# Seven-product fours in the down layers of an fp32 transformer kernel, and fours and turned chunks later in the gate/up loop

## The reference, cut to what matters

```python
def swiglu(x, w_gate, w_up, w_down):
    return (jax.nn.silu(x @ w_gate) * (x @ w_up)) @ w_down

x = x + 0.5 * swiglu(rmsnorm(x, g1), ffn1_w_gate, ffn1_w_up, ffn1_w_down)   # 2048 -> 5632 -> 2048
x = x + hybrid_mixer(rmsnorm(x, g2), ...)
x = x + 0.5 * swiglu(rmsnorm(x, g3), ffn2_w_gate, ffn2_w_up, ffn2_w_down)
return rmsnorm(x, g4)
```

## Time and profile before

| | |
|---|---|
| median of 3 runs | 2597.78 us (2594.83 to 2601.99) |
| the profiled execution's own time | 2595.44 us |
| its span | 2593.6 us |
| TensorE (PE) busy | 2576.0 us, 99% |
| VectorE (DVE) busy | 1765.2 us, 68% |
| ScalarE (ACT) busy | 1258.1 us, 49% |
| granted TensorE clock | 1.00 |
| moved by DMA | 561.53 MB, mean 217 GB/s |

### The profile page before, as it was taken

One profiled execution on the slowest core, in us unless ns is written; L12 is line 12 of the kernel. 1 busy time (PEld: TensorE's weight loads), 2 busy tenths in 40 slices (PEclk: granted clock), 3 DMA queues, 4 the chain that ended last, 5 costly groups with the idle time before them and its releaser, 6 DMA issues.

```text
span 2593.6 us, 32729 instructions
## 1 busy us (share of the span) xinstructions
PE 2576.0 (99%) x11549; PEld 2128.6 (82%) x11549; DVE 1765.2 (68%) x2077; ACT 1258.1 (49%) x1464; POOL 203.1 (8%) x345
## 2 busy tenths in 40 slices
PE   9999999999999999999999999999999999999998
PEld 8888888888788888888888888888888787888887
DVE  7766665887888865556655665555678888885554
ACT  5544554554555544444444644444454545454333
POOL 0122110000000000001100420000100000000000
PEclk9999999999999999999999999999999999999999
DMA  7788785667676776668876677665766667677654
GB/s 218 251 262 231 213 246 181 195 218 222 210 229 218 221 225 210 209 209 263 240 215 191 190 232 216 207 209 192 228 215 216 210 225 215 222 221 240 194 192 158
DMA packets 280067, 561.53 MB, mean 217 GB/s; under 512 B 22826, under 2 KB 25784, under 8 KB 279720
## 3 DMA queue, kind: packets, MB, share of 16 engines
q1 hardware_dynamic: 257120, 489.61, 60.7%
q0 software_dynamic: 22208, 70.19, 9.0%
q10 hardware_dynamic: 648, 0.52, 0.1%
HBM read 526.02 MB, written 34.22 MB: 216 GB/s over the span
## 4 chain that ended last, share of the span: by engine, by line
PE 50%; issue 42%; DMA 4%; POOL 2%; DVE 1%; ACT 0%; SPq 0%; DVEq 0%; ACTq 0%; POOLq 0%
PE acc L661 44%; DMA turn_dram<-h_turned 2%; POOL h_back L574 1%; PE acc L780 1%; PE acc L773 1%; PE acc L776 1%; PE s_ps L880 1%; DMA turn_dram<-turned_s 1%; PE o_ps L904 1%; POOL back_s L574 1%; DMA h_back<-turn_dram 0%; PE tr L796 0%; DVE wlo L1672 0%; DMA raw<-in_ffn_w_gate 0%; DMA qk<-turn_dram 0%
## 5 line engine op out<-in xcount | busy, mean ns | idle before, releaser
L1672 DVE TENSOR_TENSOR wlo<-raw,whi 128x1024 fp32r<-128x1024 f32 (+1 forms) x929 | 1098.4, 1198 | 643.0 <-ACT whi L1197 634.3
L1197 ACT ACTIVATE whi<-raw 128x1024 fp32r<-128x1024 f32 (+1 forms) x929 | 950.8, 1036 | 928.3 <-PE acc L661 659.4
L661 PE MATMUL acc<-whi,act_hi 128*128 128x512 f32 (+1 forms) x1280 | 348.5, 393 | 0.1
L661 PE MATMUL acc<-whi,act_lo 128*128 128x512 f32 (+1 forms) x1280 | 341.2, 388 | 0.0
L661 PE MATMUL acc<-wlo,act_hi 128*128 128x512 f32 (+1 forms) x1280 | 340.9, 388 | 0.0
L773 PE MATMUL acc<-whi,act_hi 128*128 128x512 f32 x1040 | 288.3, 390 | 1.6 <-ACT whi L1197 1.6
L780 PE MATMUL acc<-wlo,act_hi 128*128 128x512 f32 x1040 | 289.1, 390 | 0.7 <-DVE wlo L1672 0.2
L776 PE MATMUL acc<-whi,act_lo 128*128 128x512 f32 x1040 | 287.7, 389 | 0.0
L661 PEld LDWEIGHTS acc<-whi,act_lo 128*128 128x128 f32 x1280 | 239.2, 188 | 50.4 <-DVEq L1801 0.4
L661 PEld LDWEIGHTS acc<-wlo,act_hi 128*128 128x128 f32 x1280 | 239.3, 188 | 49.8
L661 PEld LDWEIGHTS acc<-whi,act_hi 128*128 128x128 f32 x1280 | 234.7, 188 | 44.8 <-issue 0.3
(11 more groups left out here) (335 smaller groups left out, 2324.5 us busy)
## 6 DMA issues: line engine op xcount, KB each, us to landing
raw<-in_w_in SPq DMA_DIRECT2D x280, 512.0 KB, 4.5
raw<-in_ffn_w_gate SPq DMA_DIRECT2D x176, 512.0 KB, 4.6
raw<-in_ffn_w_up SPq DMA_DIRECT2D x176, 512.0 KB, 4.3
raw<-in_ffn_w_down SPq DMA_DIRECT2D x176, 512.0 KB, 4.7
raw<-in_w_out SPq DMA_DIRECT2D x64, 512.0 KB, 4.6
turn_dram<-h_turned POOLq DMA_DIRECT2D x25, 512.0 KB, 2.9
h_back<-turn_dram POOLq DMA_DIRECT2D x100, 128.0 KB, 4.9
raw<-in_w_sg_out SPq DMA_DIRECT2D x24, 512.0 KB, 3.7
```

Source lines behind the costliest of these rows:

```text
L661: return nc.tensor.matmul(pair[:, half, 0:width], left[:, j * TILES + t, half * P:(half + 1) * P], right[:, (first_group + j) % RING, t, 0 ...
L1197: nc.scalar.activation(whi[:, slot, tiles, 0:width], source[:, tiles, 0:width], ACT.Copy).then_inc(hi_ready, 1)
L1672: nc.vector.tensor_tensor(wlo[:, slot, tiles, 0:width], split_source(m)[:, tiles, 0:width], whi[:, slot, tiles, 0:width].bitcast(F32), ALU ...
```

## The change

1. `CHUNK_ORDER`: five left, four 0, one left, one right, four 1, five right (again 20 groups). `turned_hi` and `turned_lo` of the loop move from j == 5 to j == 16 (`TURNED_AT`).
2. The down layer's four units become two pairs, (0, 1) and (2, 3), of 56 groups in `DOWN_ORDER`. k-pairs 0 to 5 of both are fours, with one left and one right group between two fours; k-pairs 6 to 21 are plain. In all, 32 plain groups and 6 fours a pair.
3. The down layer's combined activations are made in the first pair: on VectorE `combine` at j = 0, 2, 4 (two fours each) and their low part (`combined_lo`) at j = 1, 3, 5, the rounding on ScalarE (`round_four`) at j = 1, 3, 5. The last hidden chunk is split at j == 8 in place of 5.
4. At the last four of a pair `fours_out` runs, and the new `fours_added` adds its two results to `xres`; `residual_out` follows after the left part and after the right part.
5. In the first layer the exchanged chunks of x are split at j = 4 and 47 of the second pair and at j == 1 of the mixer's first unit, before TensorE's own transposes there (j == 3), and GpSimd's two loads for the layer norm (`ln_g`, `ln_b`) wait until the third of them is split. In the second layer the first three units' statistics are gathered at the group after the left part of the last pair.
6. Bookkeeping (`KINDS`, `kind_of`, `LOADS_BEFORE`) is rewritten for the two orders.

```diff
-CHUNK_ORDER = ([("left", k) for k in range(2, 6)] + four(0) + [("left", 6), ("left", 7)] + four(1)
-               + [("right", k) for k in range(2, G_D)])
+CHUNK_ORDER = ([("left", k) for k in range(2, 7)] + four(0) + [("left", 7), ("right", 2)] + four(1)
+               + [("right", k) for k in range(3, G_D)])
+TURNED_AT = len(CHUNK_ORDER) - 4
+DOWN_PAIRS = KF // TILES
+DOWN_FOURS = 6
+DOWN_ORDER = ([("left", k) for k in range(6, 12)] + [("right", k) for k in range(6, 12)] + four(0))
+for _k in range(1, DOWN_FOURS):
+    DOWN_ORDER += [("left", 11 + _k), ("right", 11 + _k)] + four(_k)
+DOWN_ORDER += [("left", k) for k in range(17, DOWN_PAIRS)] + [("right", k) for k in range(17, DOWN_PAIRS)]
...
 # GpSimd
             pool.dma_start(mfix[:], mix_fixed).then_inc(mfix_in, 16)
+            pool.wait_ge(chunk_split, 4 + 3 + 4 + 4 + FF_CHUNKS + 3)
             pool.dma_start(ln_g, sg_ln_g_2[:, :].partition_broadcast(P)).then_inc(ln_in, 16)
...
 # TensorE, ffn
-                for c in range(CHUNKS):
-                    for j in groups(KF // TILES, h_hi, h_lo, ends_by_half=4 if not first_one and c == CHUNKS - 1 else 0):
...
+                for c in (0, 2):
+                    for j in paired(DOWN_ORDER, h_hi, h_lo, down_hi, down_lo,
+                                    ends_by_half=4 if not first_one and c else 0):
+                        if c == 0 and j == 3:
+                            h_turns()
+                        if c == 0 and j == 11:
+                            pe.wait_ge(four_ready, (1 if first_one else 2 + DOWN_FOURS // 2) + DOWN_FOURS // 2)
+                        if c == 0 and j == LAST_CHUNK - 1:
                             chunk_is_split()
+                if first_one:
+                    exchanged(2)
...
             for j in groups(G_D, act_hi, act_lo):
                 if j == 3:
+                    exchanged()
+                    chunk_is_split()
                     transpose_chunk(xres, 3 * W)
...
 # ScalarE
+            def round_four(dest, source):
+                rounded[0] += 1
+                act.wait_ge(four_summed, rounded[0])
+                nc.scalar.activation(dest, source, ACT.Copy).then_inc(four_rounded, 1)
...
+                for c in (0, 2):
+                    for j in paired(DOWN_ORDER):
+                        if c == 0 and j in (1, 3, 5):
+                            if j == 1:
+                                act.wait_ge(group_used, DOWN_AT[0 if first_one else 1])
+                            round_four(down_hi[:, j - 1:j + 1], down_raw)
+                        if c == 0 and j == 8:
                             turned_hi(h_hi, KF - 4, h_back[:])
...
 # VectorE
-                        if j == 5:
-                            turned_lo(h_hi, h_lo, i * 4, h_back[:])
                         if j == LAST_FOUR:
                             fours_out()
                         if j == LEFT_DONE:
                             left_out()
+                        if j == TURNED_AT:
+                            turned_lo(h_hi, h_lo, i * 4, h_back[:])
                         if j == CHUNK_GROUPS - 1:
                             paired_gated()
...
+                def fours_added(c):
+                    for parts, cols in ((g_sb, slice(c * W, (c + 1) * W)), (h_sb, slice((c + 1) * W, (c + 2) * W))):
+                        last = nc.vector.scalar_tensor_tensor(xres[:, :, cols], parts[:], 0.5, xres[:, :, cols],
+                                                              ALU.mult, ALU.add)
+                    sum_settled(last)
+
+                for c in (0, 2):
+                    for j in paired(DOWN_ORDER):
+                        if c == 0 and j in (0, 2, 4):
+                            if j == 0:
+                                dve.wait_ge(turned, at.n["turn"] + 1)
+                            combine(h_hi[:, 2 * j:2 * j + 4, :], h_lo[:, 2 * j:2 * j + 4, :], down_x, down_raw)
+                        if c == 0 and j in (1, 3, 5):
+                            combined_lo(down_hi[:, j - 1:j + 1], down_lo[:, j - 1:j + 1], down_raw)
+                        if c == 0 and j == 8:
+                            turned_lo(h_hi, h_lo, KF - 4, h_back[:])
+                        if first_one and c and j in (4, DOWN_LAST_FOUR + 2):
+                            done = 0 if j == 4 else 1
+                            turned_lo(act_hi, act_lo, 4 * done, h_back[:], next_gain + 4 * done)
+                            at.n["ready"] += 1
+                            if not done:
+                                turn_out(1)
+                        if j == DOWN_LAST_FOUR:
+                            fours_out()
+                            fours_added(c)
+                        if j == DOWN_LEFT_DONE:
+                            residual_out(c)
+                            if first_one:
+                                turn_out(c)
+                        if not first_one and c and j == DOWN_LEFT_DONE + 1:
                             first_chunks("final", stats)
+                        if j == DOWN_GROUPS - 1 and (first_one or not c):
+                            residual_out(c + 1)
```

More of the change, by code:

```diff
@@ L19 @@
+import itertools
 import math
@@ L217, in __init__ @@
     def __init__(self):
-        self.n = dict(group=0, unit=0, job=0, chunk=0, ready=0, score=0, value=0, turn=0, paired=0, sums=0, load=0, made=0)
+        self.n = dict(group=0, unit=0, job=0, chunk=0, ready=0, score=0, value=0, turn=0, paired=0, sums=0, load=0, made=0, gated=0)
         self.turn, self.adds = None, {}
@@ L485, in ffn @@
                     at.n["unit"] += 2
-                for c in range(CHUNKS):
-                    unit(w_down, KF // TILES, c * W)
+                for c in (0, 2):
+                    for kind, k in DOWN_ORDER:
+                        if kind in ("left", "four_left"):
+                            load(w_down, k, c * W)
+                        elif kind in ("right", "four_right"):
+                            load(w_down, k, c * W + W)
+                        else:
+                            at.n["group"] += 1
+                    at.n["unit"] += 2
             sp.dma_start(fix[:, 0:P], fixed[:, 0:P]).then_inc(ident_in, 16)
@@ L785, in paired, with right_half @@
                     yield o
+                def right_half(ahead, k, half):
+                    slot = (at.n["group"] + ahead) % RING
+                    terms = plain(right, k)[half::HALVES]
+                    pe.wait_ge(hi_ready, at.target("group", ahead + 1))
+                    for bank, left_hi, left_lo, t in terms:
+                        nc.tensor.matmul(bank, left_hi, whi[:, slot, t, :], start=False, stop=False,
+                                         skip_group_check=True)
+                    for bank, left_hi, left_lo, t in terms:
+                        nc.tensor.matmul(bank, left_lo, whi[:, slot, t, :], start=False, stop=False,
+                                         skip_group_check=True)
+                    pe.wait_ge(lo_ready, at.target("group", ahead + 1))
+                    for bank, left_hi, left_lo, t in terms:
+                        last = nc.tensor.matmul(bank, left_hi, wlo[:, slot, t, :], start=False,
+                                                stop=k == order[-1][1] and t == TILES - 1, skip_group_check=True)
+                    return last
+                if ends_by_half:
+                    for ahead, (_, k) in enumerate(order[-ends_by_half:]):
+                        last = right_half(ahead, k, 0)
+                    last.then_inc(half_used, 1)
+                    for o in range(len(order) - ends_by_half, len(order)):
+                        right_half(0, order[o][1], 1).then_inc(group_used, 1)
+                        at.n["group"] += 1
+                        yield o
                 at.n["unit"] += 2
@@ L1206, in groups, with paired @@
                 at.n["unit"] += 1
-            def paired():
-                for j in range(CHUNK_GROUPS):
+            def paired(order):
+                for j in range(len(order)):
                     split_hi(AHEAD)
@@ L1214, in paired @@
                 at.n["paired"] += 1
-                at.n["load"] += CHUNK_LOADS
+                at.n["load"] += sum(kind not in ("outer", "inner") for kind, _ in order)
             def unit_ready():
@@ L1719, in paired, with combine @@
                 at.n["paired"] += 1
[L1720 to L1727 removed]
+                at.n["load"] += sum(kind not in ("outer", "inner") for kind, _ in order)
+            summed = [0]
+            def combine(hi, lo, x, combined):
+                settled(nc.vector.tensor_tensor(x, hi.bitcast(F32), lo.bitcast(F32), ALU.add))
+                a = x.rearrange("p (q t) n -> p q t n", t=TILES)
                 a11, a12 = a[:, :, 0, 0:P], a[:, :, 1, 0:P]
                 a21, a22 = a[:, :, 0, P:2 * P], a[:, :, 1, P:2 * P]
[L1730 removed]
+                c3, c5, c6, c7 = (combined[:, :, i, :] for i in range(4))
```

(18 more changed lines are left out.)

151 lines of the change are left out of this document (69 added, 82 removed).

## The result

The changed kernel takes 2575.75 us (median of 4 runs, 2573.17 to 2578.27) beside 2597.25 us for the kernel before in the same session: ratio 0.9915, 95% interval 0.9896 to 0.9934. Predicted were 2571.4 us, with a range of 2563 to 2586. The profiled execution took 2573.17 us against 2569.1 by the sum.

A forecast was written before the change was run, and what follows sets the result against it. TensorE's matmul stream, busy 99%, was taken as the bound. 2595.44 - 16.0 (loop pauses) - 16.3 (matmuls) + 2 x (2.0 + 1.0) (down-layer pauses) = 2569.1 us profiled; median 2.3 us higher, 2571.4, range 2563 to 2586.

The forecast's parts named there:

- The loop's pauses end: Both loops: new order and later turned chunk end TensorE's 16.6 us of pauses, 0.6 left; gain 16.0 us.
- The rival, that they stay because VectorE's work makes them: Loops: VectorE's work, not the exchange, makes the pauses, so they stay; 2587.4 us, chance 0.12.
- Matmuls removed: Down layers: a four has 21 matmuls for 24, so 72 fewer at 0.2267 us, 16.3 us gained.
- The start pause: Down layer's first four: its low split ends at 35.6 us, needed at 33.5; a pause of 2.0 us a layer.
- Between the down fours: Down layers: 0.2 us of pause in each of the first pair's five intervals, 1.0 us a layer.
- x + 4.9: Time between two down fours' first low splits, x until both loads land; x taken as 5.5, against TensorE's 10.20 us.
- The value named for the bound: Upper bound for pauses between down fours: at x = 6, 0.7 us in each of five intervals, 3.5 us.
- Costed at nothing: Behind the last fours: `fours_out` and `fours_added`, 5.4 us, hidden by three split groups; `residual_out` and turned chunks also without cost.
- Everything hidden: Rival for loops and down layers: no pause at all, 2564.9 us; chance 0.10.
- The ring binds: Rival: raw-buffer reuse bounds all 20 down-layer intervals; gain cancelled at 1.4 us an interval, x = 6.7; chance 0.15.
- The clock: Rival: TensorE's clock falls to 1.2 GHz in the 24 added fours, adding 114 us, 2686 us; chance 0.01.
- A sign of being wrong: Down layers: L1692, the outer sums, waiting for `raw` by more than 0.5 us in each interval would show the forecast wrong.

The follow-up runs named there:

- the five executions: Profiled executions with the changed down layers: the changed kernel twice, three kernels with edits to its loop; down-layer pauses 9.8 to 13.5 us for both layers.
- later fours: Changed kernel with 16 plain groups ahead of the down layers' first four (12 before) and six at the end (ten before); 2578.88 us.
- three groups between the fours: Changed kernel with three plain groups in four of five intervals between down-layer fours, two in the last, six at the end; 2583.90 us.
- split first and 13 ahead: Changed kernel, down layers: plain group split before waiting for a four's loads, 13 plain groups ahead of the first four, nine at the end; 2564.06 us.
- the loop part alone: Kernel before with only the loop's new group order and turned chunk at j == 16, its down layers as they were; 2579.49 us.
- half loads: Changed kernel with the down-layer fours' weight loads bringing only half their columns, 256 KB for 512 KB; 2564.26 us.

## Why the prediction was right, and which term was off

- *The loop's pauses end* (16.6, with 0.6 left): right, all of it. The reason given was right too but not the whole: the wait for the exchange does use up the lead, but the order alone takes most of it away, and without the order the second four's loads are what is late. The rival, that they stay because VectorE's work makes them, fell: VectorE's busy time in the loops is the same to 2.1 us with and without pauses (the earlier trace rows and the windows above).
- *Matmuls removed* (72 x 0.2267 = 16.3): right. Where nothing waits, a layer takes 231.20 us, 1020 x 0.2267.
- *The start pause* (2.0 a layer): right, and by the chain that was forecast (sums at 29.1 us for 29.5): 1.7 and 1.8, and 1.7 to 2.7 with a mean of 2.0 over the ten layers of the five executions, the pause at the group ahead of the four included.
- *Between the down fours* (1.0 a layer): this is the mis-sized term. It measured 3.3 and 3.0 in the first profile, and some 4 on the average of five. The step that failed is "I take 5.5" for x: the formula x + 4.9 holds to 0.05 us, but two loads 0.6 us apart took 5.2 to 6.2 in the first pair of the first layer and 5.4 to 6.8 in its second; in the second layer 5.2 to 6.0 in the first pair, but for the 7.3 beside the final gain's load, which the prediction does not name. I had added 0.6 to a median over loads that mostly stand alone, and the two close loads of the earlier trace rows come from the loop. The value named for the bound, x = 6 and 3.5 us, was nearly the truth. The second pair was costed at nothing and has 0.8 us in the first layer, where its lead is used up as well, and nothing in the second.
- *Costed at nothing*: held to 0.5 us, with ten groups for cover. With six it costs 6 us and more. At the very end, where the prediction gave the last low split 0.2 us to spare, three of the five executions lose 0.2 to 0.5 us in the second layer's last groups.
- *Everything hidden* (2564.9) did not happen, but is what the kernel reaches when the split goes first and 13 groups stand ahead: 2564.06.
- *The ring binds*: the rival lies nearer to what happened than its chance of 0.15 says. It is the mechanism; at x = 5.9 it takes 0.7 us an interval, which is less than the 1.4 that would cancel the gain. *The clock*: 1.00 throughout, in 64 fours.
- *A sign of being wrong* was met though the prediction came out: the outer sums waited for `raw` by 1.2 to 2.3 us in every interval of the first layer's first pair, where "more than 0.5 us in each interval" was to speak against it. The sign was badly set. By the prediction's own numbers an interval at x = 5.5 takes 10.4 us with 8.8 us of work in it, so VectorE stands waiting there for 1.6 us; only what goes beyond 10.20 - 8.8 = 1.4 us costs TensorE anything.

The profiled execution lay 4.1 us above the sum: 4.3 for the intervals (6.3 for 2.0) and 0.9 for the start of the kernel, less 0.6 for the loops and 0.5 for the start pauses. The forecast lay 4.3 us below the median. There two misses of opposite sign met, and that is luck: the intervals cost some 8 us for 2.0, and the loop part was worth 18.6 us for 16.0 (its profiled execution took what its median did, 2579.47 and 2579.49, while that of the kernel before lay 2.6 us below its own median; what the slower executions of the kernel before lose more was not profiled). The down part was worth about 4 us for 10.3.

## What to carry to other kernels

When an edit pairs up transfers that reuse the buffers of the pair before, write the loop from release to release as x + work, take x from rows of two transfers issued as close as they will be, look for other transfers that start beside them, and compare it with the bounding engine's time for an interval: here 0.4 us in x was 0.4 us in each interval. Where an engine waits for a transfer, put the work that does not need it ahead of the wait: one moved split was worth 9 to 10 us, more than twice what the down layers' part had brought. And count the groups left behind the last special one as cover that runs out; ten and nine were enough, six were not.

## What the runs showed that was not expected

- At three of the four longest pauses of TensorE in all these executions, of 3.04, 3.55 and 4.26 us, TensorE's granted clock fell from 1.00 to 0.50, the level of 1.2 GHz, for about 3 us, and full-width matmuls started 0.43 us apart instead of 0.227. The windows of the kernel with later fours, from the mixer's first transposes on (behind the pause of 4.26 us) and in the last groups (behind 3.04):

```profile
1174.50:1177.00 2.50, 2.41 (x10) 2.32 (x11) 2.50 (x4) 1.67 (x5) 1.08 (x2) 0.50 1.01 362
1177.00:1180.00 3.00, 3.00 (x13) 2.44 (x13) 2.56 (x5) 1.62 (x4) 0.00 (x0) 0.93 1.02 386
```

```profile
2560.20:2562.90 2.70, 2.62 (x6) 2.13 (x7) 1.68 (x9) 0.83 (x4) 0.00 (x0) 0.50 0.00 0
```

  The fourth was not followed by it. It is 3.03 us long and stands in the last groups of the kernel with three groups between the fours; its timeline row, and the window behind it, with 13 matmuls in 3.00 us:

```profile
2569.38 0.73 PE L828 MATMUL acc<-wlo,h_hi 128*128 128x512 f32 x2 [3.03 <-DVE wlo L1748]
```

```profile
2569.40:2572.40 3.00, 3.00 (x13) 2.50 (x14) 1.86 (x10) 1.27 (x6) 0.00 (x0) 1.00 0.00 0
```

  Nor were the pause of 2.51 us in the mixer of the kernel with split first and 13 ahead, and those of up to 1.8 us in the down layers. So the length of the pause alone does not settle it; where the clock falls, the pause costs more than its length: 6 matmuls in the window behind the 3.04 us took 2.6 us for 1.36.
- Half the bytes took 2 us off a pair of close loads (x of 3.3 to 4.5 for 5.2 to 6.2). The Trainium skill, "DMA: Bandwidth & Descriptors", section "Anatomy of one DMA — SWDGE (gpsimd) path", fits 2.0 us + bytes / 436 GB/s; by it, as an estimate, two of 512 KB issued together would need 4.4 us and two of 256 KB 3.2. Both came later here, issued by SyncE and 0.6 us apart: by 0.8 to 1.8 us the full ones, by 0.1 to 1.3 the halves.
- The matmul behind a pause is late as well: 0.11 us, at each pause of the changed kernel's down layers (from 959.82 to the next start at 960.15 is 0.33 us, for 0.227).
- Kernels in which TensorE stands still behind late loads scatter more from run to run than those in which it does not: 2572.96 to 2578.27 us in nine runs of the changed kernel, 2577.26 to 2579.81 in four with the loop part alone, 2563.67 to 2564.43 in four of split first with 13 ahead, and 2563.33 to 2564.36 with half loads.
